# Gated linear attention: key blocks of 32 rows by 64 columns, one key copy a tile, alternating row halves

## The reference, cut to what matters

```python
def step(S, inp):
    qc, kc, vc, lac = inp
    b = jnp.cumsum(lac, axis=1)
    b_last = b[:, -1]
    qt = qc * jnp.exp(b)
    kt = kc * jnp.exp(-b)
    attn = jnp.where(mask, jnp.einsum('bihk,bjhk->bhij', qt, kt), 0.0)
    o = jnp.einsum('bihk,bhkv->bihv', qt, S) + jnp.einsum('bhij,bjhv->bihv', attn, vc)
    kd = kc * jnp.exp(b_last[:, None] - b)
    S = jnp.exp(b_last)[..., None] * S + jnp.einsum('bjhk,bjhv->bhkv', kd, vc)
    return S, o
```

## Time and profile before

| what | value |
|---|---|
| median of three runs | 2687.17 us (2679.52 to 2690.32) |
| profiled execution | 2685.66 us |
| its span, first to last instruction | 2683.9 us |
| mean granted TensorE clock | 0.954 of 2.4 GHz |
| TensorE busy | 2543.7 us |
| VectorE busy | 1311.0 us |
| ScalarE busy | 562.9 us |

### The profile page before, as it was taken

The page is one execution under the profiler, slowest core; times in us unless marked ns, Lnnn a source line. Parts: engine busy times, 40 slices in busy tenths (PEclk is TensorE's granted clock), DMA queues, the critical chain, the costliest instruction groups (busy, mean ns, idle before and its releaser), DMA issues.

```text
span 2683.9 us, 36348 instructions
## 1 busy us (share of the span) xinstructions
PE 2543.7 (95%) x14742; PEld 2444.5 (91%) x14742; DVE 1311.0 (49%) x2006; ACT 562.9 (21%) x758; POOL 333.1 (12%) x139
## 2 busy tenths in 40 slices
PE   5999999999999989989869999999999999999997
PEld 4999999999998879879758899968999999999996
DVE  6444444444435666566536554535544444444445
ACT  3111111111102622622512333322111111101111
POOL 2112222222111000000000000001122222111210
PEclk9999999999998979979967999999999999999998
DMA  4111111111103313213343422444111111111101
GB/s 163 36 44 47 47 47 47 47 47 35 43 16 88 95 33 96 93 38 102 80 56 104 149 73 93 158 167 146 40 48 47 47 47 39 39 44 42 39 1 67
DMA packets 60929, 180.42 MB, mean 67 GB/s; under 512 B 14368, under 2 KB 21936, under 8 KB 58544
## 3 DMA queue, kind: packets, MB, share of 16 engines
q1 hardware_dynamic: 60848, 179.27, 21.6%
HBM read 171.44 MB, written 7.81 MB: 67 GB/s over the span
## 4 chain that ended last, share of the span: by engine, by line
PE 45%; DVE 3%; ACT 1%; DMA 1%; SPq 0%; issue 0%; DVEq 0%; ACTq 0%
PE ps L1503 13%; PE ps L1505 13%; PE ps L1504 13%; PE ps L1879 1%; PE ps L1832 1%; PE ps L1865 1%; DMA raw<-in_mix_tiles 1%; PE ps L1713 1%; PE ps L1521 0%; ACT pr L869 0%; PE ps L1535 0%; PE ps L1822 0%; DVE yb L988 0%; PE ps L1718 0%; PE ps L1729 0%
## 5 line engine op out<-in xcount | busy, mean ns | idle before, releaser
L1503 PE MATMUL ps<-a_hi,w_hi_sb 128*128 128x384 f32 (+1 forms) x2112 | 693.4, 328 | 18.5 <-DVE a_lo L1016 18.5
L1505 PE MATMUL ps<-a_hi,w_lo_sb 128*128 128x384 f32 (+1 forms) x2112 | 691.2, 327 | 0.0
L1504 PE MATMUL ps<-a_lo,w_hi_sb 128*128 128x384 f32 (+1 forms) x2112 | 691.0, 327 | 0.0
L572 POOL TENSOR_TENSOR w_lo_sb<-raw,w_hi_sb 128x1024 fp32r<-128x1024 f32 x135 | 332.9, 2474 | 2269.2 <-ACT w_hi_sb L600 2269.2
L1503 PEld LDWEIGHTS ps<-a_hi,w_hi_sb 128*128 128x128 f32 x2112 | 398.6, 189 | 20.5 <-DVE a_lo L1016 20.2
L1504 PEld LDWEIGHTS ps<-a_lo,w_hi_sb 128*128 128x128 f32 x2112 | 398.8, 189 | 0.3
L1505 PEld LDWEIGHTS ps<-a_hi,w_lo_sb 128*128 128x128 f32 x2112 | 398.5, 189 | 0.0
L1068 DVE TENSOR_TENSOR hf<-sil,ps 128x384 f32<-128x384 f32 x132 | 70.2, 532 | 660.7 <-ACT sil L652 660.6
L600 ACT ACTIVATE w_hi_sb<-raw 128x1024 fp32r<-128x1024 f32 x280 | 292.9, 1056 | 440.0 <-PE ps L1505 351.2
L1082 DVE SCALAR_TENSOR_TENSOR x<-ps,x 128x384 f32<-128x384 f32 (+1 forms) x528 | 279.5, 534 | 206.8 <-PE ps L1505 206.6
L1503 PE MATMUL ps<-h_hi,w_hi_sb 128*128 128x384 f32 (+1 forms) x1056 | 346.4, 328 | 0.0
(11 more groups left out here) (199 smaller groups left out, 2660.5 us busy)
## 6 DMA issues: line engine op xcount, KB each, us to landing
raw<-in_mix_tiles SPq DMA_DIRECT2D x148, 512.0 KB, 3.6
raw<-in_ffn_gate SPq DMA_DIRECT2D x44, 512.0 KB, 3.5
raw<-in_ffn_up SPq DMA_DIRECT2D x44, 512.0 KB, 3.7
raw<-in_ffn_down SPq DMA_DIRECT2D x44, 512.0 KB, 3.5
kc<-in_cache_k SPq DMA_DIRECT2D x8, 1024.0 KB, 5.0
kc<-in_cache_v SPq DMA_DIRECT2D x8, 1024.0 KB, 4.8
x<-in_x SPq DMA_DIRECT2D x2, 1536.0 KB, 9.1
out_y<-yb SPq DMA_DIRECT2D x4, 768.0 KB, 3.6
```

Of the source, the lines that this page charges most:

```text
L572: nc.gpsimd.tensor_tensor(w_lo_sb[:, slot_, :], raw[:, slot_, :], w_hi_sb[:, slot_, :].bitcast(F32), ALU.subtract)\
L1503: nc.tensor.matmul(dst, w_h, x_h, start=start, stop=False)
L1504: nc.tensor.matmul(dst, w_h, x_l, start=False, stop=False)
L1505: return nc.tensor.matmul(dst, w_l, x_h, start=False, stop=stop)
```

## The change

The key copy of a prompt tile becomes one unmasked copy, in one of two buffers by tile. kv takes 32 rows of it (chunk c) and 64 columns (head 2p+e) as the stationary block, against the 128 value columns of that head, and writes to half e of the bank's partitions, so a chunk's bank holds 2 x 128 columns instead of 4 x 128. A state update is then one 128-partition instruction a pair. In gla_a the scores alternate the halves e, in gla_b the four score-value products come first and then the state products alternate e. Bank waits stand ahead of each group of products. The sample tile keeps four masked key copies; its kv and updates take the new shapes.

```diff
-                mask = mixc(C_ROW + (0 if w == P else 4), 4)
-                for c in range(4):
-                    ins = nc.scalar.activation(kdt[0:w, c, :], bank("kdt", n, t)[0:w, 0:2 * P], ACT.Copy, scale=mask[0:w, c:c + 1])
+                if NPROMPT[n] > t * P:
+                    ins = nc.scalar.activation(kdt[:, t % 2, :], bank("kdt", n, t)[:, 0:2 * P], ACT.Copy)
+                else:
+                    mask = mixc(C_ROW + 4, 4)
...
                     for p in range(2):
-                        for e in range(2):
-                            rows = slice(64 * e, 64 * e + 64)
-                            col = t * P + (c + 1) * CH - 1
-                            ins = nc.vector.scalar_tensor_tensor(
-                                out=S[rows, (g + 1) % 8, p, :], in0=S[rows, g % 8, p, :], scalar=B[rows, p, col:col + 1],
-                                in1=bank("kv", n, t, c)[rows, (2 * p + e) * P:(2 * p + e + 1) * P], op0=ALU.mult, op1=ALU.add)
+                        ins = nc.vector.scalar_tensor_tensor(
+                            out=S[:, (g + 1) % 8, p, :], in0=S[:, g % 8, p, :], scalar=B[:, p, col:col + 1],
+                            in1=bank("kv", n, t, c)[:, p * P:(p + 1) * P], op0=ALU.mult, op1=ALU.add)
...
                 for e in range(2):
-                    rows = slice(64 * e, 64 * e + 64)
                     fill_wait(pe, "at", n, t, e)
-                    for p in range(2):
+                for p in range(2):
+                    for e in range(2):
+                        rows = slice(64 * e, 64 * e + 64)
                         ins = nc.tensor.matmul(bank("at", n, t, e)[0:w, p * w:p * w + w], qk[rows, 2 + p, cols], qk[rows, p, cols],
                                                start=True, stop=True)
-                    filled(ins, "at", n, t, e)
+                        if p:
+                            filled(ins, "at", n, t, e)
                 if prompt:
                     read_wait(pe, "kdt", n, t)
                     for c in range(P // CH):
                         fill_wait(pe, "kv", n, t, c)
-                        for p in range(2):
-                            ins = nc.tensor.matmul(bank("kv", n, t, c)[:, 2 * p * P:2 * (p + 1) * P], kdt[:, c, p * P:p * P + P],
-                                                   vt[:, t, 2 * p * P:2 * (p + 1) * P], start=True, stop=True)
-                        filled(ins, "kv", n, t, c)
+                    for p in range(2):
+                        for c in range(P // CH):
+                            rows = slice(c * CH, c * CH + CH)
+                            for e in range(2):
+                                ins = nc.tensor.matmul(bank("kv", n, t, c)[64 * e:64 * e + 64, p * P:(p + 1) * P],
+                                                       kdt[rows, t % 2, p * P + 64 * e:p * P + 64 * e + 64],
+                                                       vt[rows, t, (2 * p + e) * P:(2 * p + e + 1) * P], start=True, stop=True)
+                            if p:
+                                filled(ins, "kv", n, t, c)
...
                     for p in range(2):
                         h = 2 * p + e
-                        nc.tensor.matmul(dst[:, p * P:p * P + w], vt[:, t, h * P:h * P + P], AT[:, tile % 2, 2 * e + p, 0:w],
-                                         start=True, stop=False)
...
+                        nc.tensor.matmul(bank("o", n, t, e)[:, p * P:p * P + w], vt[:, t, h * P:h * P + P], AT[:, tile % 2, 2 * e + p, 0:w],
+                                         start=(p == 0), stop=False, skip_group_check=True)
+                if prompt:
+                    read_wait(pe, "kv", n, t, 2)
+                    parts = [(CH * c, CH, S[:, (4 * tile + c) % 8, :, :]) for c in range(P // CH)]
+                else:
+                    pe.wait_ge(s0_in, 32)
+                    parts = [(TS * b, TS, s0(b)) for b in range(NSEQ)]
+                for p in range(2):
+                    for at_, width, state in parts:
+                        last = p == 1 and at_ + width == w
+                        for e in range(2):
+                            rows = slice(64 * e, 64 * e + 64)
+                            ins = nc.tensor.matmul(bank("o", n, t, e)[:, p * P + at_:p * P + at_ + width], state[rows, p, :],
+                                                   qk[rows, p, t * P + at_:t * P + at_ + width], start=False, stop=(at_ + width == w),
+                                                   skip_group_check=True)
+                            if last:
+                                filled(ins, "o", n, t, e)
```

More of the change, by code:

```diff
@@ L777, in gla_keys @@
                 full_wait(act, "kdt", n, t)
-                mask = mixc(C_ROW + (0 if w == P else 4), 4)
-                for c in range(4):
-                    ins = nc.scalar.activation(kdt[0:w, c, :], bank("kdt", n, t)[0:w, 0:2 * P], ACT.Copy, scale=mask[0:w, c:c + 1])
+                if NPROMPT[n] > t * P:
+                    ins = nc.scalar.activation(kdt[:, t % 2, :], bank("kdt", n, t)[:, 0:2 * P], ACT.Copy)
+                else:
+                    mask = mixc(C_ROW + 4, 4)
+                    for c in range(4):
+                        ins = nc.scalar.activation(kdt[0:w, c, :], bank("kdt", n, t)[0:w, 0:2 * P], ACT.Copy, scale=mask[0:w, c:c + 1])
                 release(ins, "kdt", n, t)
@@ L1288, in gla_sample_states @@
                     full_wait(dve, "kvs", b)
+                    col = NPROMPT[2] + TS * b + TS - 1
                     for p in range(2):
-                        for e in range(2):
-                            rows = slice(64 * e, 64 * e + 64)
[L1292 to L1295, removed]
+                        ins = nc.vector.scalar_tensor_tensor(
+                            out=s0(b)[:, p, :], in0=s0(b)[:, p, :], scalar=B[:, p, col:col + 1],
+                            in1=bank("kvs", b)[:, p * P:(p + 1) * P], op0=ALU.mult, op1=ALU.add)
                     release(ins, "kvs", b)
@@ L1696, in gla_b @@
                 for e in range(2):
-                    rows = slice(64 * e, 64 * e + 64)
                     fill_wait(pe, "o", n, t, e)
                     read_wait(pe, "at", n, t, e)
[L1700 to L1704, removed]
                     for p in range(2):
                         h = 2 * p + e
-                        nc.tensor.matmul(dst[:, p * P:p * P + w], vt[:, t, h * P:h * P + P], AT[:, tile % 2, 2 * e + p, 0:w],
-                                         start=True, stop=False)
-                        if prompt:
-                            for c in range(P // CH):
-                                s = slice(t * P + c * CH, t * P + (c + 1) * CH)
-                                ins = nc.tensor.matmul(dst[:, p * P + c * CH:p * P + (c + 1) * CH], S[rows, (4 * tile + c) % 8, p, :],
-                                                       qk[rows, p, s], start=False, stop=(c == P // CH - 1))
-                        else:
-                            for b in range(NSEQ):
-                                s = slice(t * P + TS * b, t * P + TS * b + TS)
-                                ins = nc.tensor.matmul(dst[:, p * P + TS * b:p * P + TS * b + TS], s0(b)[rows, p, :],
-                                                       qk[rows, p, s], start=False, stop=(b == NSEQ - 1))
@@ L1720, in gla_b @@
-                    filled(ins, "o", n, t, e)
+                        nc.tensor.matmul(bank("o", n, t, e)[:, p * P:p * P + w], vt[:, t, h * P:h * P + P], AT[:, tile % 2, 2 * e + p, 0:w],
[6 more added lines that the diff above has]
+                    parts = [(TS * b, TS, s0(b)) for b in range(NSEQ)]
@@ L1728, in gla_sample_kv @@
                     for p in range(2):
-                        ins = nc.tensor.matmul(bank("kvs", b)[:, 2 * p * P:2 * (p + 1) * P], kdt[rows, b % 4, p * P:p * P + P],
-                                               vt[rows, 2, 2 * p * P:2 * (p + 1) * P], start=True, stop=True)
+                        for e in range(2):
+                            ins = nc.tensor.matmul(bank("kvs", b)[64 * e:64 * e + 64, p * P:(p + 1) * P],
+                                                   kdt[rows, b % 4, p * P + 64 * e:p * P + 64 * e + 64],
+                                                   vt[rows, 2, (2 * p + e) * P:(2 * p + e + 1) * P], start=True, stop=True)
                     filled(ins, "kvs", b)
```

2 lines of the change are left out of this document (1 added, 1 removed).

## The result

The changed kernel takes 2616.84 us (median of 4 runs, 2614.02 to 2618.56); the kernel before, measured beside it, 2683.35 (2679.38 to 2690.32). The ratio is 0.9753, interval 0.9734 to 0.9771. The forecast was 2643 with 2622 as its low end: the sign and the path were right, the gain (66.5 us by the medians, 42.6 forecast) was too small.

What follows compares the result with a forecast made beforehand. TensorE, busy 95% of the span, was taken as the bound. Gains of 10.4 + 9.3 + 6.2 + 5.1 + 1.0 + 10.6 = 42.6 us off 2685.66 gave 2643 us, range 2622 to 2670.

Steps and rivals of the forecast that it cites:

- Whether the shorter run still draws the drop: Dense tile behind a gla_b run: taken to stay at the lowered clock (6.86 us at 0.59), so no gain counted.
- the bound that stood there: Dense tiles behind four gla_b runs: at most 4 x 2.5 = 10 us more gain if the clock stays up.
- the rival given 15%: Dense tiles behind the shorter gla_b runs: the clock stays up, 10 us more gained, 2633 us; chance 15%.
- four row groups beside each other: 8 slots: kv of a tile: 32 records in 1.2 us, or 2.1 at the lower clock; bounds 4 and 32 slots.
- the fronts of pieces 0 and 1: Up to the first dense tile: earlier updates and norm gain 10.6 us together; 16 at the upper clock, -3 with 32 slots.
- piece 2's front: kv of tile 1 in piece 2: starts about 0.3 later, takes 2.1 us, gains 1.0.
- the 1.6 in tile 2: kv of tile 2 in pieces 0 and 1: forecast to gain 5.1 of 8.43 us, after waiting for both score masks.
- Sample kv keeps its 32-row group: Sample keys: twice as many records of half the columns, zero gain taken, up to 4 us if column halves overlap.
- the 13.2: gla_b of tiles 1 and 2, pieces 0 and 1: forecast gain 10.4 us, three tiles at the upper clock, one lower.
- the 5.5 taken: Sample tile's gla_b: 11.70 us forecast to become 5.5, a gain of 6.2 (2.7 to 6.9).
- The two halves run beside each other: Score products before the change: eight records of both halves take 0.72 us, four of one half 0.71.
- The 15.4 us of idle before it stay.: Piece 2, before kv of tile 1: TensorE's 15.4 us idle stays, set by a weight load landing 16.71 us later.

Runs made afterwards that it cites:

- Runs 1 and 2: One: kernel before with only the new gla_b, 2628.17 us. The other: changed kernel with the old gla_b, 2671.41 us.
- keys alone: Changed kernel with the old gla_b, keeping the new score order, key products, key copy and state updates: 2671.41 us, ratio 0.9940.
- run 6: Changed kernel with kv in 32-row blocks of all 128 key columns, no column halves, and the state updates and sample keys of before: 2638.17 us.
- the repeat: The changed kernel measured once more, unchanged, on the same chip as a later version: 2617.24 us, ratio 0.9760.
- halves apart: Changed kernel with all gla_b state products of the upper row half issued before those of the lower, values still first: 2641.15 us, ratio 0.9842.
- run 7: Changed kernel with VectorE's state updates as four 64-partition ones a chunk again: 2627.24 us, ratio 0.9794.
- Run 10: Changed kernel with one memory-key weight load moved ahead of the stores and the sample-state load on the same queue: 2601.20 us, ratio 0.9702.
- turns of four: Changed kernel with gla_b's state products issued in turns of four of one row half and four of the other: 2621.10 us, one run.

## Why the prediction was wrong, by its own steps

- **"Whether the shorter run still draws the drop no row decides; I take that it does."** This step failed. The four dense stretches behind gla_b of tiles 1 and 2 in pieces 0 and 1 fell from 6.86 + 11.04 + 5.72 + 9.85 = 33.5 us to 4.27 + 8.43 + 3.62 + 7.15 = 23.5: 10.0, the bound that stood there; the rival given 15% was the right one. Runs 1 and 2 put these 10.0 on gla_b. Behind the sample tile and the sample keys 5.0 more went; 4.7 of that lie behind the sample keys and come with the keys alone as well (3.06 and 5.86 us in both). Elsewhere 2.0 came back on balance: in piece 0 the dense tile behind kv went from 4.35 us at 1.00 to 5.87 at 0.71 and the last one of the stage from 4.28 to 7.04, while those behind the two fronts gained 2.2.
- **"I take four row groups beside each other: 8 slots."** This step failed: it is 4 slots, since the column halves overlap too (run 6). It was one of the two bounds. At the lower clock it is 2.1 - 1.16 = 0.94 us for each kv. Four of these stand in the fronts of pieces 0 and 1: 3.8 (VectorE's 0.32 us an update for the 0.36 taken gave 1.0 more; from the last of these updates to the dense tile it was 4.97 us where 4.6 were taken, which took 0.4 a front back; 4.0 beyond the forecast in all). In piece 2's front it is 0.9 to 1.0 of the 2.4 beyond the forecast; 0.2 to 0.4 more is a slip of the sum there (3.78 - 0.3 - 2.1 is 1.4, by the start of the next product 1.2, not 1.0); the rest was not traced. It is also behind the 1.6 in tile 2. The Trainium skill lists 32x64 among its tilings as eight independent tiles ("TensorEngine Tiling (Array Packing)", Tiling Modes); the trace agrees, 0.70 us for 32 records.
- **"Sample kv keeps its 32-row group [...]: zero taken (up to 4 if the column halves overlap)."** By the same step; they do overlap, for 3.5 us, and the clock made it 4.9.
- **gla_b.** Its slots were right to 0.1 us. 2.8 of the 13.2 come from all four tiles being at the upper clock where one was taken at the lower, again the clock. The sample tile's 4.60 us for the 5.5 taken is clock too; the repeat has 5.64.
- **"The two halves run beside each other, though the code issues all of one half first."** The row was read rightly but too widely: between two halves it holds within four records. The sum did not rest on more, since the change alternates the halves. With the halves apart, the rule of the Trainium skill cited there (strict order, "TensorE: Matmul & The Clock Gate", Part 3) is near the 3.33 us; within four records the trace disagrees.
- **The front.** Its order of events was right step for step, and its bound is VectorE, as run 7 shows. TensorE stayed at 1.2 GHz there, as the prediction took it for the outputs at its end (4.6 us).
- **"The 15.4 us of idle before it stay."** They grew to 20.0: all ahead of it became shorter and the load did not move. Run 10 shows that the load was the cause.

The low end of 2622 allowed for the clock together with the better bounds of the front, but not for the eight-wide blocks in tile 2, in piece 2 and in the samples on top of them; all came together.

## What to carry to other kernels

Small f32 products in different row groups and column halves run beside each other at one slot each, if no long turn of one block stands between them (here more than four records); price them by the slots of one block and check a moved loop for it. Most of this change is a matter of order: issuing the values first and alternating the halves, in gla_b alone, gave 56 us of the 66. Shortening a run of them can give more than its own length, where the dense work behind it ran at the lower clock; that clock is a term of the sum with its own bound, to be added to the others and not set against them. After such a change look for what now waits longest: here one weight load queued behind stores and another load held TensorE for 15 us.

## What the runs showed of the hardware

- Records of the two row halves: a half starts beside the other's last four records. 32 records take 1.98, 2.00, 2.49 and 3.33 us in turns of one, two, four and eight products (two records each) at 2.4 GHz.
- 32-row, 64-column blocks run eight wide: 32 records of 128 columns in 0.70 us, the first records of all eight blocks within 0.05 us, 16 records of 32x128 and 256 columns in 1.15, 16 with all 128 rows in 3.72.
- One more change between 128-row and 64-row products in a tile costs 0.3 us at 2.4 GHz.
- A state update of VectorE costs 0.32 us with 128 partitions and 0.36 with 64.
- In the changed kernel and its repeat every dense tile behind a 2.9 to 3.0 us gla_b ran at 1.00; in the kernel before, with keys alone and with the halves apart, the same dense work behind unpaired runs was at 0.59 to 0.83 throughout; behind the half-paired turns of four it was at 0.71 to 1.00.
